# Reordering GpSimd's start-up work and shrinking a DRAM bias table in a one-layer hybrid decoder kernel

## The chip, the cores and the metric

The kernel runs on one core of one Trainium2 chip. The metric is the device time of one execution in microseconds, the median of several runs. TensorE is called PE here, VectorE DVE, ScalarE ACT, GpSimd POOL and SyncE SP; ACT and SP also issue transfers.

## The reference, cut to what matters

One layer of a hybrid decoder is computed for 16 meta tokens, a prompt of 512 tokens, and 8 x 8 sample tokens: 592 columns in all, d_model 2048, float32. The part that matters here is the input projection with its norm, the recurrent gates, and the T5 position bias of the windowed attention:

```python
u = rmsnorm(h, norm_mix_g[l])
z = u @ w_in[l]
q, k, v, xr, gr = jnp.split(z, split_at, axis=-1)
...
bias = rel_bias.astype(jnp.float32)[rel_bucket(dist)]
s = jnp.where(mask[:, None, None], s + bias[None], -jnp.inf)
...
gate_a = jax.nn.sigmoid(einsum('btnc,ncd->btnd', xb, w_a) + b_a)
log_a = -LRU_C * gate_a * jax.nn.softplus(-lam.astype(jnp.float32))
a = jnp.exp(log_a)
mult = jnp.sqrt(-jnp.expm1(2.0 * log_a))
```

After the mixers come two norms, the output projection, and a squared-ReLU MLP of width 8192 with its residual add and the final norm.

## The kernel before, in words

**Operands.** Every product keeps float32 accuracy by splitting both operands into a high part, rounded to fp32r, and the remainder, and by multiplying high x high, high x low, low x high. Weights of the projections come in slabs of 128 x 1024 (one output tile of 128 rows, 8 input tiles). SP loads a slab into one of two raw buffers `w_raw` (L536), ACT rounds it (`w_high`, writes `w_hi`, L1008), POOL subtracts (`w_low`, writes `w_lo`, L1441). A raw buffer is free for the next slab when both have read the last one; a ring of four holds the split slabs. PE takes them at L675.

**Start.** The activations `x_raw` arrive as 16 tiles of 128 x 592. For each tile k ACT writes the high part (L1024), DVE the remainder (L1687, `scalar_tensor_tensor`), and PE multiplies it into the first two output groups, slabs 0 and 1 for k = 0 to 7, slabs 2 and 3 for k = 8 to 15. For the norm the squares of the tiles are summed: tiles 0 to 3 by POOL (`square_x`, L1451, L1454, L1455), tiles 4 to 15 by ACT (square, L1032) and DVE (add into `acc`, L1693 and L1700). ACT's square of tile k waits for DVE's add of tile k - 2 (two buffers), and its w_high of slab 2 stands behind tile 6 in its order, that of slab 3 behind tile 9. PE sums both accumulators over the partitions (`token_sums`, L701) ahead of k = 12, so it needs all of DVE's adds there. At k = 10 PE makes the bias table `gy` (L738), DVE adds its mask (L1697, in its order behind the remainder of tile 14), and ACT stores it to `gy_dram` (L1035).

**Softplus.** softplus(-lambda) is a series: DVE and ACT prepare it, and POOL does 19 dependent steps on 128 x 8 tiles (`spt`, L1465 to L1470), each waiting for the one before; the last sets `sp_ready`. POOL's order before the change is: w_low of slab 1, squares 0 and 1, the 19 steps, w_low of slabs 2 and 3, squares 2 and 3, and then the recurrent blocks.

**Recurrent blocks.** Eight blocks n follow, four slabs each. In block n DVE scales the branch out of PSUM (L1711 to L1715), ACT and DVE do the convolution (`tap0`, L1045; L1722), PE multiplies by the gate matrices (`gates`, L726) when the convolution is there, ACT does the tanhs (L1063 to L1069), the third of which reads `sp2` of the softplus, and DVE goes on to the scan and the output of the block (L1736 to L1758). The next block's convolution starts only after that. ACT's order in a block is: w_high of two slabs (for block 0 they stand ahead of the block), tap0, w_high, the GELU of the other branch, w_high, gates, the square of the result.

**Bias.** Much later in ACT's order, one transfer (L1115) reads the table back as `bias_p`, 128 partitions x 8 heads x 256, each partition at an offset one element lower than the last; 32 small ones (L1103) read it for the sample tokens. DVE waits for all of them before the first attention unit (L1822).

Of the kernel before, what the change touches and what calls it, by code (L numbers as in the profile page):

```python
# [37 lines left out]
P = 128  # L38
# [36 lines left out]
RING = 4  # L75
# [10 lines left out]
X_POOL = 4  # L86
# [125 lines left out]
def hymba_layer(nc, weights, x_t, params, consts, rel_bias, onehot, gy_mask, w_gates, cache_kt, cache_v,  # L212
                cache_k_rows, cache_v_rows, w_mlp, y_t, kv_t, conv_o, lru_o, keep_k, keep_v):
    ctx = ExitStack()
    gy_dram = nc.dram_tensor("gy_dram", [HEADS, P, GY], F32, kind="Internal")
    hid_dram = nc.dram_tensor("hid_dram", [UP, P, CW], F32, kind="Internal").ap()
    h_dram = nc.dram_tensor("h_dram", [DEPTH, P, CW], F32, kind="Internal").ap()

# [81 lines left out]
    sp2 = small("sp2", [NB])  # L300
    spt = small("spt", [4, NB])
# [29 lines left out]
    bias_p = sb("bias_p", [HEADS, 2 * P], F32, at + 6144 + 3072 + 2048)  # L331
# [18 lines left out]
    gy = sb("gy", [GY], F32, reg_h + NB * TILE + 8 * GY + 32)  # L350
# [14 lines left out]
    gy_stored = sem("gy_stored")  # L365
    bias_landed = sem("bias_landed")
# [634 lines left out]
    def _(act):  # L1001
# [19 lines left out]
        for k in range(KT):  # L1021
# [6 lines left out]
            if k >= X_POOL:  # L1028
# [1 line left out]
                if j >= 2:  # L1030
                    act.wait_ge(x_added, j - 1)
                nc.scalar.activation(sq[:, j % 2, :], x_raw[:, k, :], ACT.Square).then_inc(x_squared, 1)  # L1032
        act.wait_ge(gy_ready, 1)

        act.dma_start(gy_dram.ap(), gy[0:HEADS, :].rearrange("h (o y) -> h o y", o=1).to_broadcast([HEADS, P, GY]))\  # L1035
            .then_inc(gy_stored, 16)
        w_high(4, 0)
        w_high(5, 1)
        root(0)

        def tap0(n):

# [17 lines left out]

        def gates(n):
            act.wait_ge(gates_ready, n + 1)
            nc.scalar.activation(t_a[:, :].rearrange("p (h n) -> p h n", h=2), ps[:, 4:6, 0:LH], ACT.Tanh,  # L1063
                                 bias=half_b[:, 0, bass.ds(n, 1)], scale=0.5).then_inc(tanh_a, 1)
            nc.scalar.activation(t_x[:, :].rearrange("p (h n) -> p h n", h=2), ps[:, 6:8, 0:LH], ACT.Tanh,
                                 bias=half_b[:, 1, bass.ds(n, 1)], scale=0.5).then_inc(tanh_x, 1)

            act.wait_ge(tanh_a, n + 1)
            nc.scalar.activation(t_a[:, :], t_a[:, :], ACT.Tanh, bias=sp2[:, bass.ds(n, 1)],  # L1069
                                 scale=sp2[:, bass.ds(n, 1)]).then_inc(tau_ready, 1)  # L1070
            act.wait_ge(tau_ready, n + 1)
            nc.scalar.activation(t_s[:, :], t_a[:, :], ACT.Sqrt).then_inc(sqrt_ready, 1)
# [22 lines left out]
        def sample_bias(n):  # L1095

            own, i, b, g = n % 2, n // 2 % 2, n // 4 % 4, n // 16
            src = g * GQ * P * GY + P - 1
            if own:
                c, width, src = P + DEC_T * (4 * i + b), DEC_T, src + P  # L1100
            else:
                c, width = 0, P
            act.dma_start(bias_s[32 * b:32 * b + 32, i, g, c:c + width],  # L1103
                          bass.AP(gy_dram, src, [[P * GY, GQ], [GY - 1, DEC_T], [1, width]])).then_inc(bias_landed, 16)

        for i in range(8):
            w_high(SLABS_REC + 4 + i, i % RING)
            if i == 2:
                act.wait_ge(xr_kept, NB)
                act.dma_start(conv_o, conv_out[:, :, :, :]).then_inc(stored, 16)  # L1110
                act.wait_ge(rec_ready, NB)
                act.dma_start(lru_o, lru_out[:, :, :]).then_inc(stored, 16)

                act.wait_ge(gy_stored, 16)
                act.dma_start(bias_p[:, :, :], bass.AP(gy_dram, P - 1, [[GY - 1, P], [P * GY, HEADS], [1, 2 * P]]))\  # L1115
                    .then_inc(bias_landed, 16)
            if i >= 3:

# [312 lines left out]
    def _(pool):  # L1431
        step = Steps(pool, pool_step)

        def w_low(s, slot, free=True):

            pool.wait_ge(raw_landed[slot % RAW], s * 8 + (16 - 8 * (slot % RAW)))
            pool.wait_ge(hi_ready, s + 1)
            if free:

                pool.wait_ge(slab_used, s - (RING - 1))  # L1440
            nc.gpsimd.tensor_tensor(w_lo[slot][:, :, :], w_raw[:, slot % RAW, :].rearrange("p (k n) -> p k n", k=SLAB_K),  # L1441
                                    w_hi[slot][:, :, :].bitcast(F32), ALU.subtract).then_inc(lo_ready, 1)

        g = nc.gpsimd

        def square_x(k):

            if k % 2 == 0:
                pool.wait_ge(x_landed[k // 2], 16)
            if k == 0:  # L1450
                g.tensor_tensor(mlp_a[:, :], x_raw[:, k, :], x_raw[:, k, :], ALU.mult).then_inc(x_pool_summed, 1)  # L1451
            else:
                pool.wait_ge(x_pool_summed, k)
                step(g.tensor_tensor(mlp_b[:, :], x_raw[:, k, :], x_raw[:, k, :], ALU.mult))  # L1454
                g.tensor_tensor(mlp_a[:, :], mlp_a[:, :], mlp_b[:, :], ALU.add).then_inc(x_pool_summed, 1)  # L1455
# [4 lines left out]
        square_x(0)  # L1460
        square_x(1)

        pool.wait_ge(sp_atanh, 1)
        for d in (15, 13, 11, 9, 7, 5, 3, 1):
            step(g.tensor_tensor(spt[:, 0, :], spt[:, 0, :], spt[:, 3, :], ALU.mult))  # L1465
            step(g.tensor_scalar(spt[:, 0, :], spt[:, 0, :], 1.0 / d, None, ALU.add))
        step(g.tensor_tensor(spt[:, 0, :], spt[:, 0, :], spt[:, 1, :], ALU.mult))

        step(g.tensor_scalar(spt[:, 0, :], spt[:, 0, :], 4.0, None, ALU.mult))
        g.tensor_tensor(sp2[:, :], spt[:, 0, :], spt[:, 2, :], ALU.add).then_inc(sp_ready, 1)  # L1470
        w_low(2, 2, False)
# [51 lines left out]
        pool_base = step.base
        rec_block(0, True)
# [24 lines left out]
        for u in range(NU):  # L1549
# [4 lines left out]
            kind, i, g = UNITS[u]  # L1554
# [70 lines left out]
    def _(dve):  # L1625
# [596 lines left out]
```

## Time and profile before

| | us |
|---|---|
| median of 3 runs | 2221.93 |
| lowest and highest | 2220.57, 2222.99 |
| the profiled execution | 2223.4 |
| its span, first to last instruction | 2221.6 |
| PE busy | 2114.9 (95%) |
| DVE busy | 1576.2 (71%) |
| ACT busy | 960.6 (43%) |
| POOL busy | 366.3 (16%) |

The profiled execution took 2223.4 us, of which its span is 2221.6 us; 1.8 us lie around it. PE is busy almost throughout, so time can only change where PE waits or runs at its lower clock. All that the change touches lies in the first 100 us, but for the transfers of the bias.

### The profile page before, as it was taken

The page shows a single profiled execution, that of the slowest core. Times are in us where ns is not written, and L with a number is a line of the kernel's source. Part 1 is how long each engine was busy: PE and PEld are TensorE (multiplying, and loading weights), DVE is VectorE, ACT ScalarE, POOL GpSimd, SP SyncE. Part 2 cuts the span into 40 slices and gives each one's busy share as a digit, 9 for nine tenths or more (in the row PEclk, how much of TensorE's full clock was granted, in tenths as well). Part 3 has the DMA queues.
Part 4 walks back from the last instruction along what each step waited for, and adds up shares of the span by engine and source line. Part 5 has one row for each costly group of instructions (what it writes and reads, how often), then busy time and mean ns, then how long its engine had stood idle before and what let it go on. Part 6 is the DMA issues. An engine that isn't in the chain of part 4 may idle for free.

```text
span 2221.6 us, 38585 instructions
## 1 busy us (share of the span) xinstructions
PE 2114.9 (95%) x15424; PEld 2077.2 (94%) x15424; DVE 1576.2 (71%) x1990; ACT 960.6 (43%) x1308; POOL 366.3 (16%) x239
## 2 busy tenths in 40 slices
PE   6899999989996999999999999889999999999985
PEld 5799999869996999999999999879999999999984
DVE  6667720474347777777778777789888888888765
ACT  5344421452234334343434343455555555555453
POOL 6244443464554000000000000000000000000012
PEclk9999999999998999999999999999999999999996
DMA  5322242223331333333343434355454545454512
GB/s 175 90 81 80 81 138 93 105 95 107 98 125 50 110 123 118 126 115 129 112 142 110 145 107 137 121 195 209 164 193 167 187 163 188 162 189 162 178 53 93
DMA packets 89148, 289.66 MB, mean 130 GB/s; under 512 B 10081, under 2 KB 19721, under 8 KB 88713
## 3 DMA queue, kind: packets, MB, share of 16 engines
q1 hardware_dynamic: 77888, 269.60, 35.8%
q10 hardware_dynamic: 11112, 17.99, 2.7%
q8 instruction: 106, 1.74, 0.3%
q14 instruction: 42, 0.34, 0.0%
HBM read 238.84 MB, written 50.68 MB: 130 GB/s over the span
## 4 chain that ended last, share of the span: by engine, by line
PE 86%; DVE 6%; issue 3%; POOL 2%; DMA 1%; ACT 1%; ACTq 0%; SPq 0%; POOLq 0%; DVEq 0%
PE ps L935 61%; PE ps L675 22%; DMA w_raw<-weights 1%; DVE w_pair L1917 1%; PE ps L726 1%; PE ps L701 1%; POOL w_lo L1441 1%; DVE stat L1823 0%; DVE probs L1822 0%; DMA blk<-w_mlp 0%; ACT w_pair L1308 0%; ACT w_hi L1008 0%; DVE quad L1905 0%; DVE diff L1896 0%; DVE stat L1824 0%
## 5 line engine op out<-in xcount | busy, mean ns | idle before, releaser
L935 PE MATMUL ps<-quad,w_pair 128*128 128x288 f32 x10752 | 1447.6, 297 | 48.9 <-DVE w_pair L1917 29.0
L935 PEld LDWEIGHTS ps<-quad,w_pair 128*128 128x128 f32 x10752 | 1438.3, 190 | 58.4 <-issue 42.3
L1308 ACT ACTIVATE w_pair<-blk 128x1024 fp32r<-128x1024 f32 (+7 forms) x426 | 414.8, 975 | 547.7 <-PE ps L935 381.8
L1917 DVE TENSOR_TENSOR w_pair<-blk,w_pair 128x1024 fp32r<-128x1024 f32 (+7 forms) x426 | 477.0, 1121 | 161.4 <-ACT w_pair L1308 154.0
L675 PE MATMUL ps<-xact,w_hi 128*128 128x288 f32 (+1 forms) x2816 | 499.8, 300 | 20.7 <-POOL w_lo L1441 10.1
L675 PEld LDWEIGHTS ps<-xact,w_hi 128*128 128x128 f32 x2816 | 419.3, 190 | 24.0 <-issue 12.0
L675 PE MATMUL ps<-xact,w_lo 128*128 128x288 f32 (+1 forms) x1408 | 303.2, 297 | 0.0
L1614 POOL TENSOR_TENSOR fin_acc<-fin_acc,fin_sq 128x1152 f32<-128x1152 f32 x6 | 16.2, 2701 | 1456.2 <-ACT fin_sq L1404 1456.2
L1441 POOL TENSOR_TENSOR w_lo<-w_raw,w_hi 128x1024 fp32r<-128x1024 f32 x87 | 219.3, 2526 | 216.4 <-ACT w_hi L1008 211.1
L675 PEld LDWEIGHTS ps<-xact,w_lo 128*128 128x128 f32 x1408 | 228.4, 190 | 0.0
L1008 ACT ACTIVATE w_hi<-w_raw 128x1024 fp32r<-128x1024 f32 x88 | 92.1, 1056 | 268.0 <-PE ps L675 196.0
L1934 DVE TENSOR_TENSOR blk<-blk 128x1024 f32<-128x1024 f32 (+7 forms) x142 | 158.6, 1117 | 8.1 <-DVE w_pair L1917 0.9
L1917 DVE TENSOR_TENSOR w_pair<-w_t,w_pair 128x1024 fp32r<-128x1024 f32 (+4 forms) x71 | 81.3, 1145 | 12.8 <-ACT w_pair L1308 12.8
L1934 DVE TENSOR_TENSOR w_t<-blk 128x1024 f32<-128x1024 f32 (+4 forms) x71 | 79.1, 1114 | 3.0 <-DMA blk<-w_mlp 3.0
L1315 ACT ACTIVATE ps<-stage 128x288 f32<-128x288 f32 x120 | 47.4, 411 | 77.3 <-DVE stage L1996 64.3
L1934 DVE TENSOR_TENSOR blk<-w_t,blk 128x1024 f32<-128x1024 f32 (+4 forms) x71 | 80.4, 1132 | 0.0
L1339 ACT ACTIVATE part<-ps 128x288 f32<-128x288 f32 x71 | 29.2, 411 | 106.3 <-PE ps L935 106.3
L1970 DVE TENSOR_TENSOR part<-ps,part 128x288 f32<-128x288 f32 x71 | 32.5, 457 | 53.2 <-PE ps L935 53.1
L1308 ACT ACTIVATE w_pair<-w_t 128x1024 fp32r<-128x1024 f32 (+4 forms) x71 | 68.7, 968 | 0.0
L1979 DVE TENSOR_TENSOR part<-part 128x288 f32<-128x288 f32 x71 | 32.5, 458 | 49.3 <-ACT part L1339 48.6
L1866 DVE TENSOR_TENSOR half_out<-ps,mlp_b 128x576 f32<-128x576 f32 x16 | 12.1, 758 | 60.3 <-PE ps L675 60.1
L1722 DVE SCALAR_TENSOR_TENSOR xc<-xp,par,xc 128x616 f32<-128x616 f32 x24 | 38.8, 1617 | 19.8 <-ACT xc L1045 17.5
(257 smaller groups left out, 1339.1 us busy)
## 6 DMA issues: line engine op xcount, KB each, us to landing
blk<-w_mlp SPq DMA_DIRECT2D x228, 512.0 KB, 4.6
w_raw<-weights SPq DMA_DIRECT2D x88, 512.0 KB, 3.5
hid_dram<-stage SPq DMA_DIRECT2D x32, 576.0 KB, 5.4
quad_in<-hid_dram SPq DMA_DIRECT2D x32, 576.0 KB, 5.2
stage<-h_dram SPq DMA_DIRECT2D x30, 576.0 KB, 3.7
h_dram<-stage SPq DMA_DIRECT2D x28, 576.0 KB, 2.8
x_raw<-x_t SPq DMA_DIRECT2D x8, 592.0 KB, 9.1
h_res<-x_t ACTq DMA_DIRECT2D x4, 1152.0 KB, 10.5
```

The lines of the kernel that those rows point to most:

```text
L675: ins = nc.tensor.matmul(ps[:, 2 * buf + half, 0:width], w, act_tile(lo, kk)[:, c0 + half * width:c0 + (half + 1) * width], start=first an ...
L935: ins = nc.tensor.matmul(ps[:, i, 0:HW], w[:, k, :], quad[:, slot, lo, X_OPERAND[i], :], start=sow and opens and j == quads[0] and step == ...
L1008: nc.scalar.activation(w_hi[slot][:, :, :], w_raw[:, slot % RAW, :].rearrange("p (k n) -> p k n", k=SLAB_K), ACT.Copy).then_inc(hi_ready, 1)
L1308: nc.scalar.activation(w_half(v, i, 0), w_operand(v, i), ACT.Copy).then_inc(wh_ready, 1)
L1315: nc.scalar.activation(ps[:, i, 0:HW], home(v)[:, {1: 0, 2: 3, 5: 2, 6: 1}[i], :], ACT.Copy, scale=1.0 if i in (1, 2) else -1.0).then_inc( ...
L1339: nc.scalar.activation(part[:, 1, :], ps[:, 4, 0:HW], ACT.Copy, scale=-1.0).then_inc(n5_ready, 1)
L1441: nc.gpsimd.tensor_tensor(w_lo[slot][:, :, :], w_raw[:, slot % RAW, :].rearrange("p (k n) -> p k n", k=SLAB_K), w_hi[slot][:, :, :].bitcas ...
L1722: ins = v.scalar_tensor_tensor(xc[:, :], xp[:, j:j + LT], dcol("conv_w", n + j * NB), xc[:, :], ALU.mult, ALU.add)
L1917: v.tensor_tensor(w_half(u, i, 1), w_operand(u, i), w_half(u, i, 0).bitcast(F32), ALU.subtract).then_inc(wl_ready, 1)
L1934: v.tensor_tensor(dst, a, b, ALU.add).then_inc(w_summed, 1)
L1970: v.tensor_tensor(part[:, 2, :], bank[3], part[:, 0, :], ALU.add).then_inc(evac, 1)
L1979: v.tensor_tensor(part[:, 3, :], part[:, 1, :], part[:, 2, :], ALU.subtract).then_inc(evac, 1)
```

## The change

Four things are done. POOL's order becomes: w_low of slab 1, squares 0 and 1, w_low 2, square 2, w_low 3, square 3, w_low 4, w_low 5, then the preparation of block 0's history, then the 19 softplus steps, then block 0. ACT's wait for the softplus moves from ahead of block 0 into its `gates` (for block 0 alone), in front of the tanhs. ACT's store of the bias table moves behind w_high of slabs 4 and 5 and the root of the norm, and writes 16 copies of each head's row, not 128. `bias_p` is read by eight transfers of 16 partitions, each starting at an offset of its own, not by one of 128.

```diff
+GYR = 16
...
-    gy_dram = nc.dram_tensor("gy_dram", [HEADS, P, GY], F32, kind="Internal")
+    gy_dram = nc.dram_tensor("gy_dram", [HEADS, GYR, GY], F32, kind="Internal")
...
-        act.wait_ge(gy_ready, 1)
-
-        act.dma_start(gy_dram.ap(), gy[0:HEADS, :].rearrange("h (o y) -> h o y", o=1).to_broadcast([HEADS, P, GY]))\
-            .then_inc(gy_stored, 16)
         w_high(4, 0)
         w_high(5, 1)
         root(0)
+        act.wait_ge(gy_ready, 1)
+        act.dma_start(gy_dram.ap(), gy[0:HEADS, :].rearrange("h (o y) -> h o y", o=1).to_broadcast([HEADS, GYR, GY]))\
+            .then_inc(gy_stored, 16)
...
         def gates(n):
             act.wait_ge(gates_ready, n + 1)
+            if isinstance(n, int):
+                act.wait_ge(sp_ready, 1)
...
-        act.wait_ge(sp_ready, 1)
         rec_block(0)
...
-                act.dma_start(bias_p[:, :, :], bass.AP(gy_dram, P - 1, [[GY - 1, P], [P * GY, HEADS], [1, 2 * P]]))\
-                    .then_inc(bias_landed, 16)
+                for r in range(0, P, GYR):
+                    act.dma_start(bias_p[r:r + GYR, :, :],
+                                  bass.AP(gy_dram, P - 1 - r, [[GY - 1, GYR], [GYR * GY, HEADS], [1, 2 * P]])).then_inc(bias_landed, 16)
...
         square_x(0)
         square_x(1)
-        pool.wait_ge(sp_atanh, 1)
-        for d in (15, 13, 11, 9, 7, 5, 3, 1):
-            step(g.tensor_tensor(spt[:, 0, :], spt[:, 0, :], spt[:, 3, :], ALU.mult))
...
-        g.tensor_tensor(sp2[:, :], spt[:, 0, :], spt[:, 2, :], ALU.add).then_inc(sp_ready, 1)
         w_low(2, 2, False)
+        square_x(2)
         w_low(3, 3, False)
-        for k in range(2, X_POOL):
-            square_x(k)
+        square_x(3)
+        w_low(4, 0)
+        w_low(5, 1)
...
         def rec_block(n, first):
-            for i in (4, 5):
-                w_low(n * 4 + i, i % RING)
+            if not first:
+                for i in (4, 5):
+                    w_low(n * 4 + i, i % RING)
...
+        pool.wait_ge(sp_atanh, 1)
+        for d in (15, 13, 11, 9, 7, 5, 3, 1):
+            step(g.tensor_tensor(spt[:, 0, :], spt[:, 0, :], spt[:, 3, :], ALU.mult))
+            step(g.tensor_scalar(spt[:, 0, :], spt[:, 0, :], 1.0 / d, None, ALU.add))
...
+        g.tensor_tensor(sp2[:, :], spt[:, 0, :], spt[:, 2, :], ALU.add).then_inc(sp_ready, 1)
         step.loop(step.k)
         pool_base = step.base
         rec_block(0, True)
...
-        dve.wait_ge(bias_landed, 16 * (1 + 4 * 4 * KV))
+        dve.wait_ge(bias_landed, 16 * (P // GYR + 4 * 4 * KV))
```

## Rows read from the trace of the kernel before

**Rows 1.** Stretches: length, busy (count) of PE, PEld, DVE, ACT, POOL; granted clock; DMA share, GB/s.

```profile
34.00:40.00 6.00, 4.96 (x19) 4.64 (x20) 0.50 (x1) 0.00 (x0) 5.84 (x4) 0.51 0.53 175
...
98.00:300.00 202.00, 202.00 (x1452) 198.53 (x1451) 136.22 (x155) 83.17 (x97) 86.21 (x55) 1.00 0.27 88
```

**Rows 2.** Timeline, PE: start, us, line, what, count, idle before and releaser.

```profile
34.01 1.33 PE L675 MATMUL ps<-xact,w_hi 128*128 128x296 f32 x4 [7.63 <-POOL w_lo L1441]
...
36.86 1.30 PE L675 MATMUL ps<-xact,w_hi 128*128 128x288 f32 x4 [1.03 <-POOL w_lo L1441]
...
55.42 0.82 PE L675 MATMUL ps<-xact,w_hi 128*128 128x296 f32 x4 [0.65 <-DVE xp L1715]
...
93.44 4.48 PE L726 MATMUL ps<-xc,gate_w 128*128 128x308 f32 x8 [9.83 <-DVE xc L1722]
...
123.65 2.24 PE L726 MATMUL ps<-xc,gate_w 128*128 128x308 f32 x8
```

**Rows 3.** Timeline, POOL.

```profile
12.38 1.71 POOL L1451 TENSOR_TENSOR mlp_a<-x_raw 128x592 f32<-128x592 f32 x1
...
17.68 0.74 POOL L1465 TENSOR_TENSOR spt<-spt 128x8 f32<-128x8 f32 x1
...
30.41 0.63 POOL L1470 TENSOR_TENSOR sp<-spt 128x8 f32<-128x8 f32 x1
...
36.68 1.17 POOL L1454 TENSOR_TENSOR mlp_b<-x_raw 128x592 f32<-128x592 f32 x1
37.92 1.45 POOL L1455 TENSOR_TENSOR mlp_a<-mlp_a,mlp_b 128x592 f32<-128x592 f32 x1
...
66.75 2.40 POOL L1441 TENSOR_TENSOR w_lo<-w_raw,w_hi 128x1024 fp32r<-128x1024 f32 x1 [6.62 <-ACT w_hi L1008]
...
430.55 1.40 POOL L1552 TENSOR_TENSOR xact<-rec,xact 128x576 fp32r<-128x576 f32 x1
```

**Rows 4.** Timeline, DVE.

```profile
10.60 7.75 DVE L1687 SCALAR_TENSOR_TENSOR xact<-x_raw,par,xact 128x592 fp32r<-128x592 f32 x4 [1.39 <-ACT xact L1024]
...
20.09 0.82 DVE L1687 SCALAR_TENSOR_TENSOR xact<-x_raw,par,xact 128x592 fp32r<-128x592 f32 x1
20.84 0.77 DVE L1700 TENSOR_TENSOR acc<-acc,sq 128x592 f32<-128x592 f32 x1
...
43.61 0.76 DVE L1700 TENSOR_TENSOR acc<-acc,sq 128x592 f32<-128x592 f32 x1
...
59.38 0.75 DVE L1729 TENSOR_TENSOR gel<-ps,rb 128x576 f32<-128x576 f32 x1
67.22 2.54 DVE L1731 SCALAR_TENSOR_TENSOR gel_t<-gel_t,gel 128x576 f32<-128x576 f32 x1 [7.09 <-ACT gel_t L1057]
...
117.75 3.76 DVE L1722 SCALAR_TENSOR_TENSOR xc<-xp,par,xc 128x616 f32<-128x616 f32 x2 [0.15 <-DVE xc L1722]
...
430.57 1.39 DVE L1824 TENSOR_TENSOR stat<-stat,par 128x4 f32<-128x4 f32 x1
```

**Rows 5.** Timeline, ACT.

```profile
17.07 1.06 ACT L1008 ACTIVATE w_hi<-w_raw 128x1024 fp32r<-128x1024 f32 x1 [1.91 <-DMA w_raw<-weights]
...
22.93 1.05 ACT L1008 ACTIVATE w_hi<-w_raw 128x1024 fp32r<-128x1024 f32 x1
...
65.55 1.06 ACT L1008 ACTIVATE w_hi<-w_raw 128x1024 fp32r<-128x1024 f32 x1 [9.20 <-DMA w_raw<-weights]
...
69.79 0.69 ACT L1059 ACTIVATE gel_t<-gel_t 128x576 f32<-128x576 f32 x1 [1.30 <-DVE gel_t L1731]
...
71.34 0.75 ACT L1063 ACTIVATE t_a<-ps,half_b 128x616 f32<-128x616 f32 x1
```

**Rows 6.** DMA queues, 42 to 72 us: packets, MB, share of 16 engines.

```profile
q10 hardware_dynamic: 877, 1.35, 38.9%
```

**Rows 7.** Timeline, ACT, issue of the bias reads.

```profile
291.39 0.48 ACTq L1115 DMA_DIRECT2D bias_p<-gy_dram  x1
...
305.25 1.06 ACT L1008 ACTIVATE w_hi<-w_raw 128x1024 fp32r<-128x1024 f32 x1 [4.54 <-PE ps L675]
```

More of the change, by code:

```diff
@@ L1097, in sample_bias @@
             own, i, b, g = n % 2, n // 2 % 2, n // 4 % 4, n // 16
-            src = g * GQ * P * GY + P - 1
+            src = g * GQ * GYR * GY + P - 1
             if own:
@@ L1103, in sample_bias @@
             act.dma_start(bias_s[32 * b:32 * b + 32, i, g, c:c + width],
-                          bass.AP(gy_dram, src, [[P * GY, GQ], [GY - 1, DEC_T], [1, width]])).then_inc(bias_landed, 16)
+                          bass.AP(gy_dram, src, [[GYR * GY, GQ], [GY - 1, DEC_T], [1, width]])).then_inc(bias_landed, 16)
         for i in range(8):
@@ L1461, in _ @@
         square_x(1)
-        pool.wait_ge(sp_atanh, 1)
-        for d in (15, 13, 11, 9, 7, 5, 3, 1):
-            step(g.tensor_tensor(spt[:, 0, :], spt[:, 0, :], spt[:, 3, :], ALU.mult))
-            step(g.tensor_scalar(spt[:, 0, :], spt[:, 0, :], 1.0 / d, None, ALU.add))
-        step(g.tensor_tensor(spt[:, 0, :], spt[:, 0, :], spt[:, 1, :], ALU.mult))
-        step(g.tensor_scalar(spt[:, 0, :], spt[:, 0, :], 4.0, None, ALU.mult))
-        g.tensor_tensor(sp2[:, :], spt[:, 0, :], spt[:, 2, :], ALU.add).then_inc(sp_ready, 1)
         w_low(2, 2, False)
+        square_x(2)
         w_low(3, 3, False)
-        for k in range(2, X_POOL):
-            square_x(k)
+        square_x(3)
+        w_low(4, 0)
+        w_low(5, 1)
         def history(n):
@@ L1520, in rec_block @@
             add_rec(n, first)
+        pool.wait_ge(sp_atanh, 1)
+        for d in (15, 13, 11, 9, 7, 5, 3, 1):
+            step(g.tensor_tensor(spt[:, 0, :], spt[:, 0, :], spt[:, 3, :], ALU.mult))
+            step(g.tensor_scalar(spt[:, 0, :], spt[:, 0, :], 1.0 / d, None, ALU.add))
+        step(g.tensor_tensor(spt[:, 0, :], spt[:, 0, :], spt[:, 1, :], ALU.mult))
+        step(g.tensor_scalar(spt[:, 0, :], spt[:, 0, :], 4.0, None, ALU.mult))
+        g.tensor_tensor(sp2[:, :], spt[:, 0, :], spt[:, 2, :], ALU.add).then_inc(sp_ready, 1)
         step.loop(step.k)
```

## The prediction, as it was made blind

> **What bounds the kernel now.** I read the page first: PE is busy 2114.9 of 2221.6 us, so only PE's gaps and its slow stretches are to be had. Then the waits of PE, and the stretches: from 98 to 300 us PE is busy for all 202 us at full clock [rows 1], and behind that nothing of POOL's order or of the table is waited for. Time won or lost here is won or lost before 100 us, as the place of PE's later work. In the timeline of PE [rows 2] there are two such places.
>
> The first gap: PE has finished tile 7 and waits 7.63 us for w_lo of slab 2, then 1.03 us for slab 3, both POOL's, because POOL is in its 19 softplus steps from 17.68 to 31.04 us [rows 3]. PE comes back at half clock (0.51 granted from 34 to 40 us, which is 1.2 of 2.4 GHz [rows 1]). The second gap: after slab 7 PE waits 9.83 us for block 1's convolution [rows 2], which stands behind all of block 0 on DVE; block 0 is late because ACT's w_high of slab 6 waits 9.20 us for its load, up to 65.55, and ACT's first tanh, behind it in order, starts at 71.34 [rows 5]. That load is slow because it shares the DMA engines with the 1.5 MB table: the queue that carries it moves 1.35 MB in 30 us and takes 38.9% of the engines' time [rows 6].
>
> **The lock that decides.** DVE's remainder and its add read two SBUF operands each, and so do POOL's big operations. The rows show the two engines taking turns by whole instructions. DVE's product at 67.22 takes 2.54 us and ends at 69.76, 0.61 us after POOL's w_low (66.75 to 69.15) [rows 3, 4]; a remainder alone takes 0.82 us. A tensor_tensor is held too: 128x4 elements take 1.39 us at 430.57, and end as POOL's 1.40 us operation from 430.55 ends. In the dense stretch from 10.60 to 18.35 us DVE gets four remainders done, one per POOL instruction (7.75 us), and POOL pays: its square takes 1.71 us there and 1.17 alone. Against the small softplus steps DVE ran unhindered, a remainder at 20.09 and an add at 20.84, 1.44 us per tile with the next. So the chain before the change was the one thing on POOL that left DVE alone, and the new order puts six big instructions in its place, at the time when DVE has 11 remainders and 11 adds to do.
>
> The Trainium skill ("SBUF — State Buffer", sections "Who interferes with whom" and "Summary: rules for kernel authors") says the same of two SBUF inputs and advises to give precedence to what is on the critical path, which speaks against this change; it also counts an f32 copy such as DVE's first one into acc among those that are held, which no row here shows: the adds would then end 0.5 us later.
>
> **The front, step by step.** I take as the time that an instruction holds the lock: 2.35 us for a w_low (2.40 recorded), 1.1 and 1.37 for POOL's square and its sum (1.17, 1.45), 0.65 for DVE, 0.72 from one DVE instruction to the next [rows 3, 4]. w_hi of slab 2 is there at 18.13 [rows 5]. POOL: w_low 2 until 20.6, then square 2 and its sum with a DVE instruction between each, until 24.2. DVE has by then done tile 5's remainder only, where it was at tile 8 before. w_high 3 stood at 22.93 [rows 5]; it is behind ACT's tile 9, that behind the square of tile 8, that behind DVE's add of tile 6, now at 26.3, so w_hi 3 comes at 28.7. DVE runs free meanwhile and ends the add of tile 8 at 29.1. w_low 3 runs 29.1 to 31.5: that is where PE's first gap now ends, 5 us earlier than 36.86 [rows 2]. Square 3 and its sum take until 35.3, with one DVE instruction each; the remainder of tile 10 ends at 35.9. From there eight more, at 0.72, bring the remainder of tile 14 to 41.7; 0.5 for the mask of the table and 0.72 for the add of tile 14 make 43.0.
>
> ACT's square of tile 15 waits for the add of tile 13 (41.0), w_hi 4 is ready at 42.8, and POOL asks for w_low 4 within 0.2 us of DVE's asking for the remainder of tile 15. If DVE wins, its last add falls between w_low 4 and 5 and ends at about 46.6; if POOL wins, both lie ahead of it and it ends at 49.0. I call it even: 47.8. Before it was 44.37 (43.61 plus 0.76) [rows 4], though DVE had then waited for PE to make the table. PE has done tile 11 by 39 to 43 us and waits for this add, its sum over the partitions being due. So the 8.66 us of the first gap don't come back; they move to a new gap ahead of k = 12, and 2.2 to 4.6 us are added.
>
> PE's work from that add to slab 4 took 55.42 - 44.37 = 11.05 us at full clock. The low clock costs 1.0 us (1.33 us for four products at 34.01, against 0.82 at 55.42, and so for the next 4 to 6 us) to 3.2 us; I take 2.3. Slab 4 starts at 47.8 + 11.05 + 2.3 = 61.2, 5.7 us later than now.
>
> **The rear.** Now 15.92 us lie between slab 4 and the first tanh (55.42 to 71.34). Without the late load, the tanh follows this sequence: tap0 and the convolution 4.0 us (55.42 to 59.38), the scaling of the GELU branch 0.75 [rows 2, 4], and beside it, from 0.6 us behind the convolution, POOL's w_low 6; DVE's polynomial is held by it and ends 0.65 us behind, as at 67.22 (0.6 + 2.4 + 0.65 = 3.6 us behind the convolution); then the tanh 0.7 and w_high 7, 1.05 [rows 5]; sum 9.3 us. The load of slab 6 is issued when w_low 4 ends (45.3) and lands some 4 us later. A table of an eighth takes, at the rate of rows 6, about 192 KB x 30 / 1.35 MB = 4.3 us of its queue, and is issued near 51 us, behind it. The tanh: 61.2 + 9.3 = 70.5, 0.8 us earlier than now. DVE's chain from there to block 1's convolution is unchanged, 22.1 us (71.34 to 93.44): 92.6. PE ends slab 7 28.2 us behind the start of slab 4 (93.44 - 9.83 - 55.42 [rows 2]), at 89.4, and waits 3.2 us instead of 9.83. After 7.63 and 9.83 us of waiting PE came back at half clock, after 0.65 (at 55.42) at full; 3.2 is nearer the last, so I take full clock, with half as the bound: the gate products take 2.24 us (at 123.65 [rows 2]) and not 4.48, and the first products of slab 8 0.5 us less, 2.7 in all. PE would then reach block 2's gates 0.8 + 2.7 = 3.5 us sooner, and DVE's chain (which ends 117.75 + 3.76 = 121.5 now, 2.1 us ahead of PE's 123.65) would be there at 120.7: gain 2.9 us. From there PE is never idle [rows 1], and the place is kept.
>
> **What costs nothing.** ACT's wait for the softplus: POOL reaches the chain near 49 us, behind w_low 5 and the 0.7 us of the history; 13.4 us as now (17.68 to 31.04) make 62.5, 8 us ahead of the tanh. Behind that wait ACT has the tanhs, the square and the w_highs of slabs 8 and 9; POOL's own w_low 6 stands behind the chain, and needs the convolution (65) anyway. The eight reads: 8 x 0.48 = 3.9 us of ACT issue for 0.48 [rows 7], 3.4 us more, on an engine that idled 4.54 us before its next but two w_high for PE to free a slot; three slabs of lead on PE are the cover, and without it 3.4 us would be the price. ACT's store moves behind the root; the root is not later by it. Bytes read for the bias are the same, and DVE needs them at 412 us.
>
> **Sum.** -0.8 (rear chain) and -2.1 (clock, bounded by DVE): -2.9, say -3. The profiled execution was 2223.4 (span 2221.6), 1.5 over the median 2221.93; applied to the median: **2219.0 us**. Own range, from the even race and the low clock's bounds: 2216.5 to 2222.
>
> **Rivals.**
> (a) The lock costs less than I take, because POOL's waits fall where DVE has work, or the clock has recovered before k = 12. Every us that the last add comes sooner passes to the end. With the add at 46.6 and full clock: slab 4 at 57.7, tanh at 67.0, gain 4.3 plus up to 2.7, limited by DVE to 4.5: 2215 to 2217.4. For it: w_hi 3 is late and leaves DVE free. Against it: the four turns at 10.60. Chance 0.22.
> (b) No lock to speak of; the first gap simply closes. PE goes on at 26.4, slab 4 near 44, tanh at 53.5, gain 17.8: 2204. Against it stand all the rows above. Chance 0.08.
> (c) Slower: PE's new gap of 5 to 9 us ahead of k = 12 starts a low clock that lasts through k = 15 and slab 4. Half clock over 10 us costs 5 us; the add at 49.0 and this make slab 4 at 65.0, the tanh 74.3, 3 us later than now, and if block 1's wait also ends at low clock nothing is given back: 2225. It decides against the change once slab 4 starts after 62.1. Chance 0.15, a third of it beyond 0.2%.
> (d) The shorter table changes nothing for ACT, the load being late for another reason: then the tanh comes 15.9 us after slab 4 and the loss is 5.7: 2227.6. Against it is the queue's share [rows 6]. Chance 0.03.
>
> **Chances.** The forecast has 0.52. 0.2% is 4.4 us, about what a measurement of this kernel can tell from no change. Faster than 2217.5: (b), nearly all of (a), 0.08 of the forecast: 0.36. Slower than 2226.4: 0.08. The rest, 0.56, within. The range for 8 in 10 reaches into (a) and (c): 2213 to 2225.
>
> **What would show it.** Right: PE's wait for POOL L1441 near 34 us gone or under 3 us, and a new wait of 5 to 9 us ahead of the sums at L701 for DVE L1700; DVE's remainders between 18 and 36 us lengthened to about 2 us; w_high 6 waiting for no load; PE's wait at L726 near 3 us and at full clock. Wrong: L701 starting before 44 us (then (a) or (b)), or PE at 0.5 beyond 56 us (then (c)).

## The result and the profile after

| | before | after |
|---|---|---|
| median, us | 2220.62 | 2214.21 |
| lowest and highest, us | 2218.76, 2224.38 | 2210.93, 2217.43 |
| runs | 10 | 10 |
| profiled execution, us | 2223.4 | 2212.55 |

The ratio of after to before is 0.9971, 95% interval [0.9963, 0.9979]: the change gives 6.4 us, 0.29%. The profiled pair differs by 10.9 us, more than the medians. ACT's root of the second norm, behind all of the recurrent blocks' projections, starts at 319.83 after and at 325.89 before, 6.06 us sooner; the other 4.8 us arose behind it. The profiled execution of before lies 2.8 us above its median, that of after 1.7 us below, so these 4.8 us are taken as scatter and not as an effect. In both traces PE is busy without a gap from 98 to 300 us, so what is read below ends at 98 us.

All times of a trace are also counted from PE's first product (F), since the first loads do not land equally soon: F is 9.31 before and 10.01 after.

PE's timeline after, the lines that answer to [rows 2] (start, us, line, what, count, idle before and releaser):

```profile
31.84 0.77 PE L676 MATMUL ps<-xact,w_hi 128*128 128x288 f32 x4 [1.49 <-POOL w_lo L1443]
...
44.48 0.35 PE L702 MATMUL ps<-con,acc 128*128 128x1 f32 x2 [2.73 <-DVE acc L1705]
...
56.66 0.81 PE L676 MATMUL ps<-xact,w_hi 128*128 128x296 f32 x4 [0.65 <-DVE xp L1720]
...
88.03 3.88 PE L727 MATMUL ps<-xc,gate_w 128*128 128x308 f32 x8 [3.16 <-DVE xc L1727]
```

The 7.63 us wait for slab 2's `w_lo` is gone; the one for slab 3 is 1.49 us. A new wait of 2.73 us stands ahead of the token sums, released by DVE's last add. Slab 4 starts at 56.66, which is 46.65 behind F and was 46.11. Ahead of block 1's gates PE waits 3.16 us, where it waited 9.83, and the gates themselves take 3.88 us, 4.48 before and 2.24 at full clock [rows 2].

The stretches after (length, busy and count of PE, PEld, DVE, ACT, POOL; granted clock; DMA share; GB/s):

```profile
34.00:40.00 6.00, 4.45 (x19) 3.46 (x18) 6.00 (x7) 4.62 (x7) 1.29 (x1) 0.72 0.09 36
40.00:50.00 10.00, 7.27 (x47) 7.08 (x47) 6.83 (x14) 4.97 (x7) 7.05 (x7) 0.84 0.20 59
...
88.00:94.00 6.00, 5.97 (x25) 4.82 (x26) 3.94 (x3) 4.21 (x6) 3.21 (x5) 0.74 0.40 141
...
98.00:300.00 202.00, 202.00 (x1452) 198.54 (x1451) 133.16 (x153) 78.68 (x90) 86.22 (x55) 1.00 0.28 85
```

The low clock of 34 to 40 us is shorter than in [rows 1] (0.72 granted on the mean against 0.51), but another has come at 40 to 50 us, with 0.84 on the mean, and one lies at 88 to 94 us, about the gates.

DVE's timeline after, for [rows 4]:

```profile
22.24 1.74 DVE L1705 TENSOR_TENSOR acc<-acc,sq 128x592 f32<-128x592 f32 x1
...
29.38 2.94 DVE L1692 SCALAR_TENSOR_TENSOR xact<-x_raw,par,xact 128x592 fp32r<-128x592 f32 x1
32.24 1.74 DVE L1705 TENSOR_TENSOR acc<-acc,sq 128x592 f32<-128x592 f32 x1
...
42.72 0.82 DVE L1692 SCALAR_TENSOR_TENSOR xact<-x_raw,par,xact 128x592 fp32r<-128x592 f32 x1
43.47 0.76 DVE L1705 TENSOR_TENSOR acc<-acc,sq 128x592 f32<-128x592 f32 x1
```

A remainder lasts 2.94 us from 29.38, where POOL's w_low runs from 29.11 to 31.69; adds last 1.74 us beside POOL's squares and their sums. At 42.72 DVE and POOL start together, and DVE's remainder of tile 15 takes 0.82 and its last add, right behind it, 0.76: the last add ends at 44.23.

POOL's timeline after, for [rows 3]:

```profile
23.43 1.86 POOL L1457 TENSOR_TENSOR mlp_a<-mlp_a,mlp_b 128x592 f32<-128x592 f32 x1
29.11 2.58 POOL L1443 TENSOR_TENSOR w_lo<-w_raw,w_hi 128x1024 fp32r<-128x1024 f32 x1 [3.83 <-ACT w_hi L1009]
...
42.72 6.04 POOL L1443 TENSOR_TENSOR w_lo<-w_raw,w_hi 128x1024 fp32r<-128x1024 f32 x2 [7.42 <-ACT w_hi L1009]
...
49.02 0.23 POOL L1521 TENSOR_TENSOR spt<-spt 128x8 f32<-128x8 f32 x1
...
54.88 0.20 POOL L1526 TENSOR_TENSOR sp<-spt 128x8 f32<-128x8 f32 x1
```

It is POOL that pays there: two w_lows take 6.04 us, where one alone takes 2.40 [rows 3]. (A pair of them took 5.71 us at 31.00 before, where one DVE remainder ran between the two.) The 19 softplus steps now run from 49.02 to 55.08.

ACT's timeline after, for [rows 5, 7]:

```profile
57.45 1.04 ACT L1009 ACTIVATE w_hi<-w_raw 128x1024 fp32r<-128x1024 f32 x1
...
65.85 0.76 ACT L1065 ACTIVATE t_a<-ps,half_b 128x616 f32<-128x616 f32 x1
...
285.60 4.18 ACTq L1117 DMA_DIRECT2D bias_p<-gy_dram  x8
289.88 1.06 ACT L1009 ACTIVATE w_hi<-w_raw 128x1024 fp32r<-128x1024 f32 x1 [4.12 <-issue]
...
305.75 1.06 ACT L1009 ACTIVATE w_hi<-w_raw 128x1024 fp32r<-128x1024 f32 x1 [4.29 <-PE ps L676]
```

The w_high of slab 6, at 57.45, waits for no load (9.20 us before [rows 5]). The first tanh starts at 65.85, 9.19 us behind slab 4, where 15.92 lay between them. The issue of the eight bias reads takes 4.18 us, and the w_high at 305.75 still waits 4.29 us for PE, nearly as long as the one at 305.25 did before [rows 7].

The transfers issued from 40 to 72 us, KB each and median us from issue to landing, say why the first tanh is sooner. After:

```profile
w_raw<-weights SPq DMA_DIRECT2D x4, 512.0 KB, 3.5
gy_dram<-gy ACTq DMA_DIRECT2D x1, 192.0 KB
```

And before:

```profile
gy_dram<-gy ACTq DMA_DIRECT2D x1, 1536.0 KB
w_raw<-weights SPq DMA_DIRECT2D x3, 512.0 KB, 18.0
```

In the median a slab of 512 KB lands 3.5 us behind its issue after, and 18.0 us before.

### The profile page after: what moved, and what is told of

Read it like the earlier page. It is cut to its first block, busy times and chain, and to the rows that moved or that the text cites. A ratio compares the mean times of both kernels' runs of the same rounds, so it can differ in the third digit from the quotient of the medians.

```text
span 2210.7 us, 38593 instructions
## 1 busy us (share of the span) xinstructions
PE 2115.4 (96%) x15424; PEld 2077.6 (94%) x15424; DVE 1582.9 (72%) x1990; ACT 959.9 (43%) x1308; POOL 360.8 (16%) x239
## 3 DMA queue, kind: packets, MB, share of 16 engines
q8 instruction: 106, 1.74, 0.3%
## 4 chain that ended last, share of the span: by engine, by line
PE 86%; DVE 8%; issue 3%; ACT 1%; DMA 1%; POOL 1%; ACTq 0%; SPq 0%; POOLq 0%; DVEq 0%
PE ps L936 61%; PE ps L676 22%; DVE w_pair L1922 1%; PE ps L702 1%; PE ps L727 1%; DVE acc L1705 0%; ACT w_pair L1310 0%; DVE xact L1692 0%; DVE stat L1828 0%; DVE probs L1827 0%; DMA w_raw<-weights 0%; DVE blk L1939 0%; DVE xc L1727 0%; DVE w_t L1939 0%; DVE quad L1910 0%
## 5 line engine op out<-in xcount | busy, mean ns | idle before, releaser
L1984 DVE TENSOR_TENSOR part<-part 128x288 f32<-128x288 f32 x71 | 32.5, 457 | 48.5 <-ACT part L1341 47.8
```

What stands on the lines that cost most here:

```text
L1984: v.tensor_tensor(part[:, 3, :], part[:, 1, :], part[:, 2, :], ALU.subtract).then_inc(evac, 1)
```

## The experiments

Each was compared with the kernel before on the same chip. The columns are the end of DVE's last add and the start of slab 4, both from F; the time from that add to slab 4; from slab 4 to the first tanh; PE's wait ahead of block 1's gates; the length of those gates; the second root from F; the median; the ratio to before with its interval. The first seven come from one profiled execution each, the last two from all runs. In e6, e8 and e10 PE takes tile 12 ahead of the sums, 1.6 us of products at full clock, so their column from the add to slab 4 holds 1.6 us less work than in the other rows.

| | last add | slab 4 | add to slab 4 | to tanh | PE waits | gates | 2nd root | median | ratio |
|---|---|---|---|---|---|---|---|---|---|
| before | 35.06 | 46.11 | 11.05 | 15.92 | 9.83 | 4.48 | 316.58 | 2220.62 | 1 |
| after | 34.22 | 46.65 | 12.43 | 9.19 | 3.16 | 3.88 | 309.82 | 2214.21 | 0.9971 [0.9963, 0.9979] |
| a0, after once more | 34.34 | 49.78 | 15.44 | 9.19 | 3.18 | 3.67 | 313.03 | 2214.37 | 0.9969 [0.9956, 0.9982] |
| e1, table alone | 35.82 | 48.41 | 12.59 | 9.24 | 3.22 | 4.03 | 311.75 | 2215.15 | 0.9972 [0.9963, 0.9981] |
| e2, order alone | 34.24 | 48.85 | 14.61 | 9.17 | 7.12 | 4.48 | 317.23 | 2219.28 | 0.999 [0.9981, 0.9999] |
| e3, late store alone | 36.41 | 48.98 | 12.57 | 9.24 | 7.20 | 4.20 | 316.50 | 2219.60 | 0.9995 [0.9986, 1.0004] |
| e4, two squares fewer | 31.31 | 46.43 | 15.12 | 9.18 | 3.17 | 4.03 | 310.08 | 2213.03 | 0.9965 [0.9954, 0.9977] |
| e5, w_high 4 early | 38.09 | 52.41 | 14.32 | 9.17 | 3.15 | 3.73 | 315.46 | 2221.06 | 0.9998 [0.9989, 1.0007] |
| e6, e4 and later sums | 31.28 | 43.73 | 12.45 | 9.19 | 3.16 | 3.23 | 307.27 | 2211.05 | 0.9959 [0.9945, 0.9972] |
| e8, later sums | 34.21 | 46.61 | 12.40 | 9.18 | 3.17 | 4.47 | 310.99 | 2213.57 | 0.9968 [0.9956, 0.998] |
| e9, PE kept busy | 34.29 | 46.58 | 12.29 | 9.18 | 0.45 | 2.34 | 309.35 | 2212.91 | 0.996 [0.9948, 0.9973] |
| e10, e6 kept busy | 31.77 | 42.43 | 10.66 | 9.18 | 0.42 | 2.34 | 305.93 | 2210.35 | 0.9946 [0.9934, 0.9958] |

### a0: the changed kernel once more

No edit. It shows how far two traces of one kernel differ.

> The changed kernel as it is, to see how its trace varies. All theories: first 300 us as in the first trace within 1 us (slab 4 starts some 46.6 us after PE's first product, block 1's gates wait some 3.2 us), ratio 0.995 to 0.999. If PE's clock behind the 3.2 us wait is not the same here, that level is a matter of where the wait falls, not of its length.

PE's timeline in a0:

```profile
44.35 0.56 PE L702 MATMUL ps<-con,acc 128*128 128x1 f32 x2 [2.71 <-DVE acc L1705]
...
59.53 0.81 PE L676 MATMUL ps<-xact,w_hi 128*128 128x296 f32 x4 [0.65 <-DVE xp L1720]
...
90.92 3.67 PE L727 MATMUL ps<-xc,gate_w 128*128 128x308 f32 x8 [3.18 <-DVE xc L1727]
```

The stretch behind the add in a0, with the columns of the stretches above:

```profile
44.00:54.00 10.00, 9.65 (x42) 9.68 (x43) 1.91 (x8) 0.90 (x2) 8.58 (x20) 0.50 0.43 122
```

The add comes at the same place (34.34 against 34.22 from F), the wait ahead of the sums is the same 2.71 us, but the granted clock is 0.50 for the whole 10 us behind it, and slab 4 starts 3.1 us later than in the first trace (49.78 against 46.65). The medians are 0.2 us apart. So the columns up to the last add, to the tanh and the waits repeat within 0.2 us, and those that hold PE's work behind the sums do not within 3 us. The 1 us expected was too narrow.

### e1: the short table alone

```diff
+GYR = 16
...
-    gy_dram = nc.dram_tensor("gy_dram", [HEADS, P, GY], F32, kind="Internal")
+    gy_dram = nc.dram_tensor("gy_dram", [HEADS, GYR, GY], F32, kind="Internal")
...
```

To the kernel before: the 16 copies and the eight reads, with POOL's order and the place of the store as before.

> The kernel before with the short table and its eight reads alone; POOL's order, ACT's order and the place of the store stay. Theory T (the table gives nearly all, POOL's order gives nothing): slab 4 starts as before (46.1 us after PE's first product), the first tanh 9.3 us behind it, so 6.5 us sooner than before; 6 to 8 us gained in all, as much as the whole change or up to 1.5 us more. Theory R (POOL's order is worth the 8.66 us it was made for, the table little): under 3 us gained.

PE's timeline in e1:

```profile
34.24 1.33 PE L676 MATMUL ps<-xact,w_hi 128*128 128x296 f32 x4 [6.79 <-POOL w_lo L1443]
...
57.95 0.81 PE L676 MATMUL ps<-xact,w_hi 128*128 128x296 f32 x4 [0.65 <-DVE xp L1717]
...
89.38 4.03 PE L727 MATMUL ps<-xc,gate_w 128*128 128x308 f32 x8 [3.22 <-DVE xc L1724]
```

ACT's first tanh in e1, from its timeline:

```profile
67.19 0.76 ACT L1064 ACTIVATE t_a<-ps,half_b 128x616 f32<-128x616 f32 x1
```

The first gap is still there (6.79 us for slab 2), and yet the tanh comes 9.24 us behind slab 4, PE waits 3.22 us ahead of block 1's gates, and the ratio is that of the whole change (0.9972 against 0.9971).

The front itself scatters. before, e1 and e3 have the same order of POOL and the same first gap, and yet their last adds end at 35.06, 35.82 and 36.41 from F and slab 4 starts at 46.11, 48.41 and 48.98, where 46.1 was expected of e1: behind the first gap PE's half clock lasted to about 40 us in before, 42 in e1 and 45 in e3, and e1 has a second stretch at half clock behind the sums (0.50 granted at 49 to 52 us), with no wait ahead of them. Among these three, before is the quickest.

### e2: the order alone

```diff
-GYR = 16
+GYR = 128
```

To the changed kernel: all 128 copies, one read; POOL's order, ACT's wait and the late store stay.

> The changed kernel with the table written 128 times over and read by one transfer: the order of POOL, the place of the store and ACT's wait are the changed ones. Theory T: the front gains nothing; the load of slab 6 is issued before the store and is not late, but that of slab 7, issued behind it, shares the engines with 1.5 MB and lands some 10 us late or more, so the first tanh comes 11 to 15 us behind the start of slab 4; gain between -1 and 4 us. Theory R: 5 us or more.

PE's timeline in e2:

```profile
58.05 0.82 PE L676 MATMUL ps<-xact,w_hi 128*128 128x296 f32 x4 [0.66 <-DVE xp L1720]
...
93.36 4.48 PE L727 MATMUL ps<-xc,gate_w 128*128 128x308 f32 x8 [7.12 <-DVE xc L1727]
```

ACT's timeline in e2:

```profile
67.22 0.76 ACT L1065 ACTIVATE t_a<-ps,half_b 128x616 f32<-128x616 f32 x1
...
85.17 1.06 ACT L1009 ACTIVATE w_hi<-w_raw 128x1024 fp32r<-128x1024 f32 x1 [3.85 <-DMA w_raw<-weights]
```

The tanh is at 9.17 behind slab 4, not at 11 to 15 as expected: the store, issued later, does not reach slab 6's load. It reaches slab 8's: the w_high at 85.17 waits 3.85 us for its load, and PE waits 7.12 us ahead of block 1's gates. The late load has moved, and order and late store together give 0.1%, at the edge of what the interval can tell from nothing.

### e3: the late store alone

```diff
+        w_high(4, 0)
+        w_high(5, 1)
+        root(0)
         act.wait_ge(gy_ready, 1)
-        w_high(4, 0)
-        w_high(5, 1)
-        root(0)
```

To the kernel before, with its 128 copies.

> The kernel before with only ACT's store of the table moved behind w_high of slabs 4 and 5 and the root; it still writes 128 copies. If the size of the store is what counts (theory T): the load of slab 6 is issued at nearly the same moment as the store, and that of slab 7 some 2 us behind it; the wait for loads moves to block 1, as in the run with the order alone, where PE waited 7.1 us for block 1's gates; gain 0 to 3 us. If its place is what counts: the same 6 us as with the short table alone.

ACT's timeline in e3:

```profile
66.52 0.75 ACT L1063 ACTIVATE t_a<-ps,half_b 128x616 f32<-128x616 f32 x1
...
84.09 1.06 ACT L1008 ACTIVATE w_hi<-w_raw 128x1024 fp32r<-128x1024 f32 x1 [3.48 <-DMA w_raw<-weights]
```

The same picture as e2: the first tanh 9.24 us behind slab 4, then 3.48 us of waiting for slab 8's load, 7.20 us of PE's. The place of the store decides only which block is late; what helps is to store fewer bytes.

### e4: two squares fewer on POOL

```diff
-X_POOL = 4
+X_POOL = 2
...
         w_low(2, 2, False)
-        square_x(2)
         w_low(3, 3, False)
-        square_x(3)
```

To the changed kernel; ACT and DVE take the squares and sums of tiles 2 and 3 instead.

> The changed kernel with the squares and sums of tiles 2 and 3 on ACT and DVE, not on POOL: four big POOL instructions fewer, two DVE adds more (0.72 us each) in the front. If the lock sets DVE's last add (theory L): the last add ends some 3.2 us sooner and slab 4 starts 2 to 4 us sooner than in the changed kernel, and the total is that much less. If DVE's own work sets it: slab 4 1.4 us later.

PE's timeline in e4:

```profile
41.17 0.55 PE L702 MATMUL ps<-con,acc 128*128 128x1 f32 x2 [3.68 <-DVE acc L1703]
...
56.03 0.81 PE L676 MATMUL ps<-xact,w_hi 128*128 128x296 f32 x4 [0.65 <-DVE xp L1718]
```

The stretch about the sums in e4:

```profile
40.00:52.00 12.00, 10.83 (x52) 10.86 (x53) 2.72 (x9) 1.70 (x3) 10.02 (x23) 0.57 0.38 106
```

The last add ends 2.9 us sooner (31.31 against 34.22), though DVE has two adds more to do: POOL's four operations on two operands had cost it more than that. Slab 4 is at 46.43, though, 0.2 us sooner only; the clock granted from 40 to 52 us is 0.57, and the way from the add to slab 4 takes 15.12 us. The time is 2213.03, 1.2 us below after's, and the intervals overlap: of the 2 to 4 us expected nothing is shown.

### e5: w_high of slab 4 sooner, so that POOL gets its turn

```diff
-        w_high(4, 0)
+            if k == KT - 2:
+                w_high(4, 0)
         w_high(5, 1)
```

To the changed kernel. POOL's w_low 4 then asks for the lock ahead of DVE's last three instructions.

> The changed kernel with ACT's w_high of slab 4 moved up, to behind the square of tile 14, so that POOL's w_low 4 asks for the lock ahead of DVE's last instructions. Theory L (the lock): DVE loses one w_low, so its last add ends some 2.4 us later (36.6 us behind PE's first product, not 34.3), and slab 4 starts that much later at equal clock. If DVE does not wait for a POOL instruction that asks while DVE's own are queued back to back: last add at 34.3 to 35.3 as before.

DVE's timeline in e5:

```profile
42.42 2.46 DVE L1706 TENSOR_TENSOR acc<-acc,sq 128x592 f32<-128x592 f32 x1
44.80 2.90 DVE L1693 SCALAR_TENSOR_TENSOR xact<-x_raw,par,xact 128x592 fp32r<-128x592 f32 x1
47.63 0.76 DVE L1706 TENSOR_TENSOR acc<-acc,sq 128x592 f32<-128x592 f32 x1
```

The add of tile 14 takes 2.46 us and the remainder of tile 15 2.90; the last add ends at 38.09 from F, 3.9 us later than in after. PE waits 8.01 us for it, slab 4 starts 5.8 us later, and the whole gain is gone (0.9998). The add was expected 2.4 us later, for one w_low. It lost two turns, to w_low 4 and to w_low 5, and a low clock behind the sums came on top that is longer than in after's first trace (14.32 us from the add to slab 4, against 12.43). That is the losing side of the race of which the forecast and rival (c) speak, though not the whole of (c): slab 4 starts at 52.41 from F, where (c)'s 65.0 makes 55.7. POOL's being ahead at w_low 4 costs 6.9 us (2221.06 against 2214.21, medians of two comparisons; by the two ratios 6.0).

### e6 and e8: the sums one tile later

```diff
-            if k == KT - 4:
+            if k == KT - 3:
```

PE takes the token sums ahead of k = 13, not 12. e8 is after with this edit, e6 is e4 with it.

> As the run with two squares, and PE multiplies tile 12 ahead of the sums over the partitions, not behind them. PE's wait there falls from 3.7 to 2.1 us. Theory C (the low clock behind PE's wait costs what the earlier add gained): with the shorter wait the stretch from last add to slab 4 falls from 15.1 us to 10.5 to 13.5, and the total is 2 to 5 us under the changed kernel. If the wait alone counts and the clock is as in the run with two squares: 1.6 us under that run.

> The changed kernel with tile 12 multiplied ahead of the sums. PE's wait of 2.7 us there falls to 1.1 us. Theory C: slab 4 starts 1.6 us sooner at equal clock, and PE's clock does not fall there, so slab 4 is 45 us behind PE's first product and not 46.7 to 49.8; total 2 to 4 us under the changed kernel. If the low clock comes from something else than this wait: 1.6 us at most.

PE's timeline in e6:

```profile
41.44 0.35 PE L702 MATMUL ps<-con,acc 128*128 128x1 f32 x2 [2.05 <-DVE acc L1703]
...
53.64 0.81 PE L676 MATMUL ps<-xact,w_hi 128*128 128x296 f32 x4 [0.65 <-DVE xp L1718]
```

e6 has slab 4 at 43.73, 2.9 us sooner than after: here the earlier add is passed on. The wait ahead of the sums is 2.05 us. Of the 2.7 us by which e6's way from the add to slab 4 is shorter than e4's (12.45 against 15.12), 1.6 are tile 12, which now lies ahead of the sums, and 1.1 are clock. The medians differ by 2.0 us and the intervals overlap, so no gain of e6 over e4 is shown.

e8 changes nothing that can be seen in the time (46.61, 0.9968), and its wait did not fall to the 1.1 us expected: it is 2.62. The products ahead of it were quicker. Tile 10 took 1.7 us in e8 and 3.1 in after, at half clock (0.50 granted at 37 to 39 us), so PE reached the sums as early with one tile more. The low clock then came behind the wait as in after (0.50 at 46 to 51 us).

### e9 and e10: PE's gaps filled with products that nobody reads

```diff
+        def fill(n, kk, bank):
+            for _ in range(n):
+                nc.tensor.matmul(ps[:, bank, 0:HA], act_tile(0, 0)[:, META:META + P], act_tile(0, kk)[:, META:META + HA], start=True, stop=True)
...
+                fill(18, 8, 6)
                 pe.wait_ge(con_landed, 16)
...
         group(3, 6, 2, 1)
+        pe.wait_ge(tanh_x, 1)
+        fill(21, 8, 6)
         gates(1)
```

e9 is after with both (the first ahead of the sums, the second ahead of block 1's gates), e10 is e6 with 13 and 21. The products are extra work; nothing is left out.

> The changed kernel with products of no use in PE's two waits: 18 (2.4 us) ahead of its wait for the last add, 21 (2.8 us) ahead of that for block 1's convolution. Theory C (the low clock comes from PE's waits of 2 to 3 us, and costs time in the front): full clock from the last add to slab 4, so this stretch takes 11 to 11.5 us and not 12.4 to 15.4, and slab 4 starts 45 to 46 us behind PE's first product; block 1's gates take 2.24 us; the total is 2 to 5 us under the changed kernel. If the low clock has another cause: no gain, and up to 0.7 us lost where a filling product is late.

> The kernel with two squares moved and tile 12 ahead of the sums, with 13 products of no use (1.7 us) ahead of the wait for the last add and 21 (2.8 us) ahead of block 1's gates. Theory C: full clock up to slab 4, which starts 42 to 43 us behind PE's first product (43.7 without the filling); total 1 to 3 us under that kernel. Otherwise the same as that kernel.

PE's timeline in e9:

```profile
43.78 0.35 PE L702 MATMUL ps<-con,acc 128*128 128x1 f32 x2 [0.19 <-issue]
...
55.97 0.82 PE L676 MATMUL ps<-xact,w_hi 128*128 128x296 f32 x4 [0.65 <-DVE xp L1726]
...
87.38 2.34 PE L727 MATMUL ps<-xc,gate_w 128*128 128x308 f32 x8 [0.45 <-DVE xc L1733]
```

PE's timeline in e10:

```profile
40.67 0.35 PE L702 MATMUL ps<-con,acc 128*128 128x1 f32 x2 [0.20 <-issue]
...
51.24 0.81 PE L676 MATMUL ps<-xact,w_hi 128*128 128x296 f32 x4 [0.65 <-DVE xp L1724]
...
82.64 2.34 PE L727 MATMUL ps<-xc,gate_w 128*128 128x308 f32 x8 [0.42 <-DVE xc L1731]
```

Ahead of block 1's gates the filling works: they take 2.34 us, not 3.88, and the low clock of the rear is gone in both. That it is PE's gap that brings the low clock there is shown by this.

Ahead of the sums it does not keep the clock up. PE reaches them without idling (0.19 us), and yet the clock falls behind them, in e9 (0.72 granted from 46 to 52 us) and in e10 (0.72 from 42 to 48). From the add to slab 4 e9 takes 12.29 us, hardly less than after's first trace (12.43) and 3.1 less than its second (15.44). e10's 10.66 is the same length once tile 12 is counted in (12.3). So slab 4 at 46.58 missed the 45 to 46 expected of e9. The sums themselves are 20 products of one column, but they are not cause enough: in before the same 20 were followed by full clock. What makes the clock fall there stays open.

e10 is the fastest kernel of the study: 2210.35 us, 0.9946, that is 10.8 us below before, and its interval lies wholly under after's, though not quite under a0's. How much of it the filling gives is not shown: e9's interval overlaps after's, and e10's overlaps e6's.

## Why the prediction was right, and where it was not

The time forecast was 2219.0, with 2213 to 2225 as the range; 2214.21 lies in the range, but below the own range (2216.5 to 2222) and just below rival (a)'s 2215 to 2217.4. It is inside only because the range was stretched into (a), and (a), with a chance of 0.22, is what happened: the last add came sooner than forecast and passed that on. The prediction's own signs say so too. The wait ahead of the sums is 2.73 us, not 5 to 9, and L702 starts 34.47 us from F, which is 43.8 in the times of before and just under the 44 named as the sign of (a) or (b). ((a)'s 2217.4 limits its gain to 4.5 us by DVE, where the forecast adds 2.1 us to the gain at the tanh; with (a)'s 4.3 that makes 6.4, as was measured.) By its terms:

**The rear, right.** From slab 4 to the first tanh 9.3 us were forecast; eleven traces show 9.17 to 9.24. PE's wait was to be 3.2 us and is 3.16. That the late load of slab 6 was the table's doing is shown by e1 and by the landing time (3.5 against 18.0 us). Rival (d) is out.

**The order gives nothing, right.** The first gap's 8.66 us did not come back: in after, PE waits 0.44 and 1.75 us for remainders, 1.49 for slab 3, 1.55 at the table and 2.73 ahead of the sums, 7.96 in all. DVE became what PE waits for, as forecast. With the new order slab 4 starts at 46.65, 49.78 and 48.85 (after, a0, e2), with the old at 46.11, 48.41 and 48.98 (before, e1, e3), and e1, without the order, has the ratio of after. Rival (b), no lock, is out by DVE's 2.94 us remainder and by e5. The Trainium skill ("SBUF — State Buffer", section "Who interferes with whom") calls the pair of ports that DVE shares with GpSimd an exclusive lock. The trace agrees: the remainder at 29.38, 0.27 us behind w_low 3, ends at 32.32, 0.63 us behind the end of w_low 3 (31.69), so that all of its work lies behind POOL's.

The prediction left open whether DVE's first copy into `acc` is held as well. It is, in a0 and in e9. In a0's timelines of DVE and POOL:

```profile
18.73 2.69 DVE L1698 COPY acc<-sq 128x592 f32<-128x592 f32 x1
18.70 2.40 POOL L1443 TENSOR_TENSOR w_lo<-w_raw,w_hi 128x1024 fp32r<-128x1024 f32 x1 [0.52 <-ACT w_hi L1009]
```

In after the copy starts 0.08 us ahead of w_low 2 and takes 0.46 us, and the next remainder pays (2.97 from 19.34). The last add is the same for it within 0.12 us.

**The tie, the step that failed.** The forecast took the race at w_low 4 as even and put the last add at 47.8, with 46.6 if DVE won and 49.0 if POOL did. It ended at 44.23, 3.6 us sooner, or 34.22 from F instead of the 38.5 that 47.8 makes. Up to there the steps were close: w_low 3 from 29.11 (forecast 29.1), the add of tile 14 done at 42.79 (43.0), w_low 4 and the remainder of tile 15 both at 42.72. (Counted from F, these steps came 0.7 to 0.9 us sooner than forecast, and the other 3.4 of the 4.3 us are the tie.) Then DVE got two turns in a row where strict turns by instruction, on which both prices of the forecast rest, leave it one. Every other place of the front had shown such turns.

Nor was it a matter of chance. All eight traces with ACT's w_high 4 in this place (after, a0, e2, e4, e6, e8, e9, e10) have the two starts within 0.01 us of each other, then 0.82 and 0.76 us for DVE's two and 6.02 to 6.05 us for the pair of w_lows. Both sides set out from the same event, DVE's add of tile 13 (done at 40.91): ACT's square of tile 15 and w_high 4 on one, DVE's own next three on the other.

Why DVE has both turns stays open. That POOL's recorded start lies ahead of its first read would have to mean some 0.7 us here, and POOL was served first where it started only 0.27 us (29.11) or 0.03 us (18.70 in a0) ahead of DVE. The other side of the race was priced well: when POOL is ahead (e5), the add ends at 38.09 from F, and the forecast's 47.8 to 49.0 make 38.5 to 39.7.

**The clock behind the sums, a term mis-sized.** 2.3 us of low clock were forecast between the add and slab 4, with bounds of 1.0 and 3.2, on top of 11.05 us at full clock. after's first trace has 1.38 (12.43 less 11.05), the second 4.39, above the bound. It scatters from run to run. The base does so too: e1, with no wait ahead of the sums, has 12.59.

**The clock at block 1, wrong.** PE was to come back from 3.2 us of waiting at full clock; the gates take 3.2 to 4.5 us in the kernels with that wait. The 2.1 us expected of it came as 0.6 (4.48 less 3.88). e9 shows that it is the gap: filled but for 0.45 us, the gates take 2.34.

**The softplus, mis-sized without effect.** 13.4 us were forecast, 6.06 measured: the small steps last 0.20 to 0.24 us, mostly, against 0.63 in [rows 3], where DVE was busy with instructions on two operands beside them. They end 10.8 us ahead of the first tanh (forecast 8), so nothing hangs on it.

**The eight reads, right.** 4.18 us of issue (3.9 forecast), hidden under ACT's wait for PE. No run takes them by themselves.

So the sum of the forecast, +5.7 at slab 4, -6.6 in the rear, -2.1 by the clock, was in the first trace +0.54, -6.73 and -0.6, which is -6.8 at the second root; in the second trace the front has +3.7, and the root is 3.6 us sooner. The medians say -6.4. The forecast was 3.4 us too careful. In the first trace the front came out 5.2 us better than forecast, 3.4 of them by the tie, and the clock at block 1 took 1.5 us of it back.

## What to carry to other kernels

A store that multiplies a small table goes over the same DMA engines as the loads that the engines wait for: cutting its copies gave the whole 6 us, and moving it only chose another load to be late. Before work is moved up on GpSimd, count the DVE instructions with two SBUF operands that stand beside it, and find the one place where both ask at once ahead of a deadline: here its outcome was worth 6 to 7 us. Two paths that leave from one event and meet again are no coin toss: here they came out the same in all eight traces. A short wait of TensorE may be filled with products that nobody reads. That kept the clock up ahead of block 1's gates and not behind the token sums, so it has to be tried at each place. And a single trace of each kernel is not enough to price a stretch at low clock: slab 4 moved by 3 us between two traces of one kernel.

## What the runs showed of the hardware that was not expected

- Behind a wait of about 3.2 us PE's clock fell to half for all or part of the gates (3.23 to 4.47 us against 2.24), and it stayed at full when all but 0.42 to 0.45 us of the wait was filled (2.34).
- The length of a low stretch is not a property of the kernel: the same kernel had 12.43 and 15.44 us from the add to slab 4, the same 2.7 us wait ahead of both.
- An f32 copy of DVE with one SBUF operand (128x592) is held by a w_low as well: 2.69 and 2.67 us where it started 0.03 and 0.05 us behind it (a0, e9), 0.46 us where it started ahead (after).
- Small POOL steps are slowed by a busy DVE as well: the 19 steps of 128 x 8 took 13.4 us beside DVE's dense stretch and 6.06 where DVE was mostly idle; the one slow step there (0.58 us at 49.66) lies beside an instruction of DVE's on two operands (0.69 us at 49.48).
- The lock need not alternate: at 42.72 DVE had two instructions done (0.82 and 0.76 us) while POOL's pair of w_lows stretched to 6.04 us, and so in eight traces of eight.
- A store of 1.5 MB in small pieces made 512 KB loads land in 18.0 us, where they land in 3.5 beside a store of 192 KB.
